# Zeros written at another place, fetched results added by VectorE in a block of its own, and decays of the odd mixer by selectors

## The reference

```
h = x
for layer in (0, 1):                      # first stack
    h += 0.5 * rmsnorm(swiglu(rmsnorm(h)))
    h += rmsnorm(even_mixer(..) if layer == 0 else odd_mixer(..))
    h += 0.5 * rmsnorm(swiglu(rmsnorm(h)))
# second stack, layer 0: modulation (silu(c) @ ada_w), differential attention with
#   rotary q and k over context and latent tokens, dense swiglu of width 3584
# second stack, layer 1: modulation, Fourier mixer, mixture of 8 experts, top 2, width 3584
return rms_norm(x, final_g)
```

```
seg = exp(where(tri, acum[:, :, :, None] - acum[:, :, None, :], -inf))
```

## Time and profile before

| | us |
|---|---|
| median of 3 runs | 2762.97 (2759.33 to 2765.16) |
| the profiled execution | 2765.94 |
| its span | 2764.1 |
| PE busy | 2637.2 (95%) |
| DVE busy | 2058.1 (74%) |
| ACT busy | 1682.6 (61%) |
| POOL busy | 177.5 (6%) |
| mean granted TensorE clock | 0.983 of full speed |

### The profile page before, as it was taken

How to read it: one execution, slowest core, us unless ns; L and a number is a source line. 1 busy time by engine, 2 the same in 40 slices (tenths; PEclk the granted TensorE clock), 3 DMA queues, 4 the chain that set the end, 5 groups by cost and what they waited for, 6 DMA issues and landing times.

```text
span 2764.1 us, 35036 instructions
## 1 busy us (share of the span) xinstructions
PE 2637.2 (95%) x12512; PEld 2162.0 (78%) x12512; DVE 2058.1 (74%) x2379; ACT 1682.6 (61%) x2188; POOL 177.5 (6%) x199
## 2 busy tenths in 40 slices
PE   7999899999999999999986999999999999999997
PEld 6888787888887777888765888788888878888885
DVE  4556667777757765564655785799999999999998
ACT  4446645454457765453552444578788887878885
POOL 2000000000000000004210000200000000000023
PEclk9999999999999999999998999899999999999999
DMA  8555217768744336543148884599999999999995
GB/s 289 183 168 175 92 32 281 240 221 308 243 163 137 122 107 205 183 154 136 46 144 306 309 312 161 178 372 370 378 371 366 387 358 382 367 384 372 367 386 193
DMA packets 284459, 687.41 MB, mean 249 GB/s; under 512 B 13348, under 2 KB 21824, under 8 KB 284352
## 3 DMA queue, kind: packets, MB, share of 16 engines
q1 hardware_dynamic: 266176, 618.65, 62.7%
q0 software_dynamic: 18176, 67.32, 6.8%
HBM read 670.19 MB, written 15.73 MB: 248 GB/s over the span
## 4 chain that ended last, share of the span: by engine, by line
PE 83%; DVE 9%; ACT 4%; issue 4%; DMA 1%; POOL 0%; DVEq 0%; SPq 0%; ACTq 0%
PE ps L2494 25%; PE ps L2496 25%; PE ps L2495 25%; DVE w_lo L1600 3%; PE ps L2642 2%; ACT w_hi L848 1%; PE ps L2726 1%; DVE xt L2376 1%; DVE xn L1679 1%; PE ps L2934 1%; DVE h L1684 1%; PE ps L2957 0%; PE ps L3107 0%; DMA scr<-in_ada_w 0%; DVE act_lo L1668 0%
## 5 line engine op out<-in xcount | busy, mean ns | idle before, releaser
L1600 DVE TENSOR_TENSOR w_lo<-w_raw,w_hi 128x1024 fp32r<-128x1024 f32 x1158 | 1412.1, 1238 | 426.9 <-ACT w_hi L848 395.8
L848 ACT ACTIVATE w_hi<-w_raw 128x1024 fp32r<-128x1024 f32 x1158 | 1211.6, 1057 | 818.0 <-PE ps L2496 817.5
L2494 PE MATMUL ps<-w_hi,act_hi 128*128 128x512 f32 (+1 forms) x3424 | 1350.1, 394 | 75.0 <-DVE w_lo L1600 59.9
L2496 PE MATMUL ps<-w_lo,act_hi 128*128 128x512 f32 (+1 forms) x3424 | 1324.2, 387 | 0.0
L2495 PE MATMUL ps<-w_hi,act_lo 128*128 128x512 f32 (+1 forms) x3424 | 1322.8, 386 | 0.0
L2494 PEld LDWEIGHTS ps<-w_hi,act_hi 128*128 128x128 f32 x3424 | 648.3, 189 | 223.8 <-DVE w_lo L1600 76.2
L2496 PEld LDWEIGHTS ps<-w_lo,act_hi 128*128 128x128 f32 x3424 | 647.9, 189 | 132.6
L2495 PEld LDWEIGHTS ps<-w_hi,act_lo 128*128 128x128 f32 x3424 | 649.2, 190 | 125.0 <-issue 2.9
L1591 DVE SCALAR_TENSOR_TENSOR scr<-scr,small 128x1024 f32<-128x1024 f32 x98 | 125.3, 1278 | 0.0
L1006 ACT ACTIVATE act_hi<-ps 128x512 fp32r<-128x512 f32 (+1 forms) x87 | 62.5, 719 | 64.2 <-PE ps L2642 64.2
L1725 DVE TENSOR_TENSOR act_lo<-ps,act_hi 128x512 fp32r<-128x512 f32 (+1 forms) x87 | 74.0, 850 | 34.7 <-ACT act_hi L1006 34.7
(11 more groups left out here) (509 smaller groups left out, 1457.7 us busy)
## 6 DMA issues: line engine op xcount, KB each, us to landing
w_raw<-in_moe_w SPq DMA_DIRECT2D x337, 1024.0 KB, 7.1
scr<-in_ada_w POOLq DMA_DIRECT2D x48, 1024.0 KB, 6.3
w_raw<-in_ffn_w_gate SPq DMA_DIRECT2D x44, 1024.0 KB, 5.1
w_raw<-in_ffn_w_up SPq DMA_DIRECT2D x44, 1024.0 KB, 5.3
w_raw<-in_ffn_w_down SPq DMA_DIRECT2D x44, 1024.0 KB, 5.0
w_raw<-in_ff_w SPq DMA_DIRECT2D x42, 1024.0 KB, 5.3
w_raw<-in_odd_w_in SPq DMA_DIRECT2D x20, 1024.0 KB, 5.1
w_raw<-in_even_w_in SPq DMA_DIRECT2D x14, 1024.0 KB, 5.2
```

What stands on the lines that cost most here:

```text
L848: act.activation(w_hi[:, g % SPLITS, 0:c * width], w_raw[:, s % RING, o:o + c * width], ACT.Copy).then_inc(hi_done, 1)
L1600: dve.tensor_tensor(w_lo[:, g % SPLITS, 0:c * width], w_raw[:, s % RING, o:o + c * width], w_hi[:, g % SPLITS, 0:c * width].bitcast(F32), ...
L2494: pe.matmul(out_ap, hi, whi, start=start, stop=False)
L2496: return pe.matmul(out_ap, hi, wlo, start=False, stop=stop)
```

## The change

Constants and tiles: `ZEROED` counts nine transfers instead of three, `STORED_AT = 12` is new, `eid` has a 13th entry, `pick` (128 x 64) and `cumr` (128 x 128), both fp32r, are new, some small tiles shrink, `decays_twice` is `sg[:, 0:128]`.

**Zeros.** POOL writes them behind the context's root, ahead of the rotation of keys and queries, from a quarter of a MB of zeroed `lev`. ACT's wait goes.

```diff
             pool.tensor_tensor(rstd[:, 4:6], ..., ALU.pow).then_inc(da_rstd, 1)
+            zeros = lev[:, 0:4, :].rearrange("p c n -> p (c n)")
+            link(pool.memset(zeros, 0.0))
+            for blocks in [rows_in[b:b + 2] for b in range(1, MAX_BLOCKS - 1, 2)] + [rows_in[MAX_BLOCKS - 1:]] + [
+                    rows_out[b:b + 2] for b in range(N_EXPERTS - 2, MAX_BLOCKS, 2)]:
+                flat = blocks.rearrange("b p n -> (b p n)").rearrange("(q j n) -> q j n", q=P, n=BANK)
+                pool.dma_start(flat, bc_mid(zeros, flat.shape[1])).then_inc(rows_moved, 16)
...
-            pool.wait_ge(alo_done, ALO_DENSE)
-            pool.memset(xt[:, 0:DM], 0.0).then_inc(rope_link, 1)
-            pool.wait_ge(rope_link, n(rope_link))
-            for i in range(2):
-                half = rows_in[i * MAX_BLOCKS // 2:(i + 1) * MAX_BLOCKS // 2].rearrange("b p n -> p b n")
-                pool.dma_start(half, bc_mid(xt[:, 0:DM], MAX_BLOCKS // 2)).then_inc(rows_moved, 16)
-            rest = rows_out[N_EXPERTS - 1:].rearrange("b p n -> p b n")
-            pool.dma_start(rest, bc_mid(xt[:, 0:DM], MAX_BLOCKS - N_EXPERTS + 1)).then_inc(rows_moved, 16)
             modulation(1)
```

```diff
+                for k in range(2):
+                    ins = dve.scalar_tensor_tensor(decays_twice[:, 64 * k:64 * k + 64].rearrange("p (b n) -> p b n", b=TB),
+                                                   two(T_DT), -1.0, bc_mid(work[:, 0:32], TB), ALU.mult, ALU.mult)
+                ins.then_inc(dl_g, 1)
+                for k in range(2):
+                    dve.tensor_copy(pick[64 * k:64 * k + 64, :], ident[64 * k:64 * k + 64, 64 * k:64 * k + 64])
...
+                link(dve.tensor_copy(cumr[:], ps[:, 6, 128:256]))
+                dve.tensor_tensor(cumr[64:P, :], ps[64:P, 6, 128:256], cumr[64:P, :].bitcast(F32), ALU.subtract).then_inc(og_la, 1)
...
-                def rows(q, bank):
+                def rows(g, q, bank):
-                    pe.wait_ge(og_la, n(og_la))
+                    pe.wait_ge(og_la, 1)
                     pe.matmul(ps[:, bank, :], identr[:], bc_mid(negr[:], 4), start=True, stop=False)
-                    pe.matmul(ps[:, bank, :], ones, sg[:, 512 * m:512 * m + 512], start=False, stop=True).then_inc(og_R, 1)
+                    for i in range(4):
+                        head = 32 * T + 8 * g + 4 * m + i
+                        ins = pe.matmul(ps[:, bank, i * P:(i + 1) * P], pick[:, head:head + 1].to_broadcast([P, P]), cumr[:],
+                                        start=False, stop=i == 3)
+                    ins.then_inc(og_R, 1)
...
+                pe.matmul(ps[:, 6, 128:256], decays_twice, tri, start=True, stop=True).then_inc(dl_gc, 1)
```

```diff
+                    if s == moe_from + STORED_AT:
+                        sp.wait_ge(mo_y, b + 1)
+                        sp.dma_start(rows_out[bass.ds(b - 1, 1)][0], mo_ye).then_inc(rows_back, 16)
...
-            pool.wait_ge(rows_io, n_blocks * 32)
+            pool.wait_ge(rows_back, last * 16)
...
             for tb in range(TB):
-                step(pool.tensor_scalar(y_first[:, tb, :], y_first[:, tb, :], p_gate[:, tb:tb + 1], None, ALU.mult))
-                step(pool.tensor_scalar(y_second[:, tb, :], y_second[:, tb, :], p_gate[:, 2 + tb:3 + tb], None, ALU.mult))
-                step(pool.tensor_tensor(y_first[:, tb, :], y_first[:, tb, :], y_second[:, tb, :], ALU.add))
-                step(pool.tensor_tensor(y_first[:, tb, :], y_first[:, tb, :], wbc[:], ALU.mult))
-                step(pool.tensor_tensor(h[:, tb, :], h[:, tb, :], y_first[:, tb, :], ALU.add))
+                pool.tensor_scalar(y_first[:, tb, :], y_first[:, tb, :], p_gate[:, tb:tb + 1], None, ALU.mult).then_inc(mo_base, 1)
...
+                def fetched(tb):
+                    y = y_first[:, tb, :]
+                    dve.wait_ge(mo_base, tb + 1)
+                    dve.scalar_tensor_tensor(y, y_second[:, tb, :], p_gate[:, 2 + tb:3 + tb], y, ALU.mult, ALU.add).then_inc(mo_link, 1)
+                def fetched_scaled(tb):
+                    y = y_first[:, tb, :]
+                    dve.wait_ge(mo_link, 2 + 2 * tb)
+                    dve.tensor_tensor(y, y, wbc[:], ALU.mult).then_inc(mo_link, 1)
+                def fetched_added(tb):
+                    dve.wait_ge(mo_link, 3 + 2 * tb)
+                    dve.tensor_tensor(h[:, tb, :], h[:, tb, :], y_first[:, tb, :], ALU.add)
...
+                def moved_and_fetched(i):
+                    if i == GATHERED_AT - 1:
+                        dve.wait_ge(ro_act, 5)
+                        fetched(0)
+                    if i == GATHERED_AT:
+                        fetched_scaled(0)
+                    moved(i)
+                    if i == FF_STEPS - 1:
+                        fetched_added(0)
+                        fetched(1)
+                    if i == FF_STEPS:
+                        fetched_scaled(1)
+                        fetched_added(1)
...
-                with dve.Fori(0, n_blocks) as b:
+                with dve.Fori(0, last) as b:
                     start_blocks(n, b)
-                    gated(FF2, 1, beside)
+                    gated(FF2, 1, moved)
                     lo_ahead(2)
                     end_blocks(n)
+                gp[0], ahead[0], n.at = first_gran, first_ahead, first_at
+                start_blocks(n, last)
+                gated(FF2, 1, moved_and_fetched)
+                lo_ahead(2)
```

More of the change, by code:

```diff
@@ L604, in _ @@
                     sp.wait_ge(rows_moved, SCATTERED)
-                    for half in (slice(0, BANK), slice(BANK, DM)):
-                        sp.dma_start(mo_rows[:, half], rows_in[1][:, half]).then_inc(rows_io, 16)
+                    sp.dma_start(mo_rows, rows_in[1]).then_inc(rows_io, 16)
             sp.wait_ge(mo_ids, n(mo_ids))
@@ L1734, in gated @@
                         hidden(i - 1)
-                    if beside and i in (CONTEXT_AT, GATHERED_AT):
+                    if beside and i:
                         beside(i)
@@ L2110, in odd @@
                 link(dve.scalar_tensor_tensor(dtw[:, T_DT, :], dtw[:, T_X, :], 0.0, dtw[:, T_LN, :], ALU.max, ALU.add))
-                dve.scalar_tensor_tensor(two(T_A), two(T_DT), -1.0, bc_mid(work[:, 0:32], TB), ALU.mult, ALU.mult).then_inc(dl_g, 1)
+                dve.scalar_tensor_tensor(two(T_A), two(T_DT), -1.0, bc_mid(work[:, 0:32], TB), ALU.mult, ALU.mult)
+                for k in range(2):
[4 more added lines that the diff above has]
+                    dve.tensor_copy(pick[64 * k:64 * k + 64, :], ident[64 * k:64 * k + 64, 64 * k:64 * k + 64])
                 lo(1)
@@ L2430, in experts @@
+                last = dve.value_load(eid[0:1, 12:13], min_val=N_EXPERTS - 1, max_val=N_EXPERTS + MAX_EXTRA - 1)
+                first_gran, first_ahead, first_at = gp[0], ahead[0], dict(n.at)
+                with dve.Fori(0, last) as b:
+                    start_blocks(n, b)
+                    gated(FF2, 1, moved)
                     lo_ahead(2)
                     end_blocks(n)
-                dve.wait_ge(ro_act, 5)
+                gp[0], ahead[0], n.at = first_gran, first_ahead, first_at
@@ L2433, in experts @@
+                start_blocks(n, last)
+                gated(FF2, 1, moved_and_fetched)
+                lo_ahead(2)
+                n.block = None
                 dve.wait_ge(ctx_in, 48)
-                dve.wait_ge(mo_base, n(mo_base))
                 dve.wait_ge(mo_end, n(mo_end))
@@ L3007, in odd @@
                 pe.matmul(ps[:, 6, 0:64], tri, dtw[:, T_A, :], start=True, stop=True)
-                pe.matmul(ps[:, 6, 64:128], ones, dtw[:, T_A, :], start=True, stop=True).then_inc(dl_gc, 1)
+                pe.matmul(ps[:, 6, 64:128], ones, dtw[:, T_A, :], start=True, stop=True)
+                pe.matmul(ps[:, 6, 128:256], decays_twice, tri, start=True, stop=True).then_inc(dl_gc, 1)
                 for g in range(3):
@@ L3018, in beside_x @@
                                 pe.wait_ge(og_e, 4 * g)
-                            rows(0, 4)
-                            rows(1, 5)
+                            rows(g, 0, 4)
+                            rows(g, 1, 5)
                             pe.wait_ge(cv_act, CV + 2 * (3 + g))
@@ L3040, in beside_z @@
                                 pe.wait_ge(og_lo, 2 * g - 1)
-                            rows(2, 4)
+                            rows(g, 2, 4)
                             from_state(g)
@@ L3046, in beside_z @@
                                 pe.wait_ge(og_lo, 2 * g)
-                            rows(3, 5)
+                            rows(g, 3, 5)
                         if k == 3:
@@ L3058, in odd @@
                 pe.wait_ge(og_e, 12)
-                rows(0, 4)
-                rows(1, 5)
+                rows(3, 0, 4)
+                rows(3, 1, 5)
                 pe.wait_ge(proj_out, 8 + 11)
@@ L3081, in odd @@
                 pe.wait_ge(og_lo, 6)
-                rows(2, 4)
-                rows(3, 5)
+                rows(3, 2, 4)
```

(1 more changed line is left out.)

57 lines of the change are left out of this document (22 added, 35 removed).

## The result

The changed kernel takes 2712.28 us (median of 4 runs, 2709.26 to 2714.96) against 2761.15 for the kernel before (4 runs, 2758.75 to 2765.16): ratio 0.9818, 95% interval 0.9807 to 0.983, that is 48.9 us less. The forecast was 2716.3, or 46.7 less than a kernel before at 2762.97. The profiled execution took 2714.96, span 2712.8: 51.3 less than the span before.

The account below looks back on a forecast made before the run. PE bounds the kernel, matmuls being 83% of the span. Zeros -29.3, odd decays -10.7 and fetched results -6.7 sum to -46.7 us, from the runs' median 2762.97 to 2716.3 us; range 2707 to 2733.

Parts of the forecast that it names:

- Zeros, -29.3: Dense stage start: ada_w page lands in time, PE's 27.7 us wait and 1.6 of slow clock go; ends 24 and 30.
- The price 0 at the new place: Behind the context's root, from about 1067 us: zeros cost PE nothing, the seven-page weight ring covering them; upper end 21 us.
- 31 us for the zeros, or 52 beside the weights: New place: 8704 KB take 31 us with the engines alone, 52 with weights at 334 GB/s in all.
- my rule, 1 us for each beyond 31: New place: where the weight ring's cover is gone, each us of zeros beyond 31 costs PE 1 us.
- rival D: New place: zeros shut weights out, running under 114 GB/s, kernel slower than before; 2784 us at 90 GB/s; chance 0.03.
- Odd decays, -10.7: Odd mixer: four single-pass selector matmuls replace DVE products and an f32 matmul, shortening PE's work and a stall; ends -2, -13.
- my -3.6, -2.5 and +1.2: Behind the odd mixer's third group: stall gone 3.6 us, slow clock gone 2.5, ACT's late copy of x costs 1.2.
- Rival A: Odd mixer: selector matmuls run at f32's rate, four taking 0.86 us; total gain 40 us, 2723 us; chance 0.2.
- Fetched results, -6.7: Last expert block: POOL's arithmetic moves to DVE, regaining 10.7 us of PE waits and losing 4.0; ends -10.7, -3.
- 10.7 less 3.0 for the rest of the new work: Last block: 10.7 us regained; 1.3 lost at step 5, 1.4 at step 6, 0.3 from POOL's two multiplies.
- Rival C: Last block: POOL's two remaining multiplies hold DVE 7.9 us, leaving this gain at 0 to 1 us; 2722 us; chance 0.1.
- part 3: Last expert block: the fetched results done by DVE instead of POOL, forecast at -6.7 us.

Follow-up runs that it names:

- e2_decays: Kernel before with only the odd decays changed, made by the turned product and selectors: 2749.8 us, 13.2 less.
- experiment 9: Changed kernel with the 16 DVE products put back and PE waiting for two of them behind the third group: 2720.1 us, ratio 0.9844.
- Experiment 11: Changed kernel with last block's rows stored at page 8 instead of 12, six DVE instructions paired at steps 3, 4 and 6: 2710.9 us, ratio 0.9803.
- experiment 4: Kernel before with the same three transfers of zeros issued behind the first two ada_w pages instead of in front: 2755.4 us, 7.6 less.
- experiment 6: Changed kernel with each of the nine transfers of zeros issued twice, 17.8 MB instead of 8.9: 2713.8 us, ratio 0.9827.
- experiment 5: Kernel before with the same three transfers of zeros at about the same time, issued from SP's queue instead of POOL's: 2739.9 us, 21.7 less.

## Why the prediction was right, step by step

**Zeros, -29.3.** The stretch gave 29.1, and 29.8 in the kernel with this part alone. The page was in time, the 27.7 and the slow clock behind them went; the 3.93 us were nine matmuls and not ten, so the slow clock was worth 1.9, not 1.6. The price 0 at the new place held, but by another way than I had worked out, and that is luck. I took 31 us for the zeros, or 52 beside the weights. That 52 holds the weights of 41 us only; 334 GB/s less the 204 of the weights leaves 130, and makes it 68 us. They flowed for some 70 us, the issues alone over 63, with POOL standing still for 6.3 to 11.4 us before the next. By my rule, 1 us for each beyond 31, that is 39 us of idle; PE had none. Rule and rival D both priced slow zeros as if weights were shut out for as long, but beside them the weights landed in 6.7 to 7.9 us by the median: a slow transfer leaves more to the others. At 8.9 MB in some 70 us, 127 GB/s and not far above D's 114, PE lost nothing, and neither with twice the bytes.

**Odd decays, -10.7.** 10.4 in the profiled pair, 10.7 in e2_decays. A group takes 34.05 us instead of 35.72: 1.67 each, 5.0 in three, as forecast. Behind group three a wait alone makes 5.5 (experiment 9); my -3.6, -2.5 and +1.2 give 4.9. ACT's copy of x was 1.12 late for 1.2. Rival A's price was 6.7, measured 6.3; it failed on the rate alone. The selector matmul took 0.098 for the 0.11 that I took from 32 columns. The Trainium skill, "TensorE: Matmul & The Clock Gate", section "Wait — 56ns, not 53.3ns?", puts warm bf16 matmuls of 128 columns 56 ns apart; that does not carry over to these fp32r matmuls with a new stationary each, which the trace has 98 ns apart.

**Fetched results, -6.7.** Measured 6.2 to 6.3, and two misses, of 3.1 and of 2.6 us, nearly cancel in it. DVE found everything ready at step 4, so its new wait cost nothing. The end cost 4.1 where I had put 1.0. PE already waited 1.6 for DVE there before the change, so the pair behind the last w_lo went on the path whole (2.4 of waiting; I had set it against the last transposes only), and behind the longer wait the slow clock took 1.7 more, a term that I did not have. Experiment 11 takes both back. Up to the last weight matmul the block is 10.3 us shorter (130.9 to 120.5 behind the eviction), where 10.7 less 3.0 for the rest of the new work, 7.7, was forecast. The new work cost little there: 1.7 of waits over an ordinary block's 0.8, of which 1.1 at step 5 for 1.3 and 0.6 for the pair at step 6 for 1.4. So taking POOL's arithmetic away gave about 12 by estimate (10.3 and 1.7), more than the 10.7 that I had from the list of waits, which shows only 8.8 of the 10.3 (a wait is counted from the end of a pipelined matmul, 0.39 behind its start where the next could start after 0.23). Small slips of mine: 11.3 less 0.8 is 10.5, not 10.6; the 1.21 of the earlier trace rows is a median, and one w_lo in that line took 2.05; rows 16 give 120.83 and not 120.87.

Rival C: DVE is not shut out by the multiplies that stay. The Trainium skill, "SBUF — State Buffer", section "SBUF: two separate sides", would have it locked out by their read of SBUF for a whole instruction, 4.0 us here; the rows agree by two w_lo in six, lengthened by 0.7 and 0.8 us, and disagree by the rest (1.21 to 1.23).

**The rest.** 46 of the 48.9 us are in the three stretches. Of the 5.5 between the profiles beyond them 3.2 are slow spells that only one of them has, 2.9 lie where the lost clock is 3.3 less, and -0.7 stand in front of the odd mixer. The forecast of 46.7 for the three parts is nearer to their 45.8 than the sum of its terms deserves. Whether the 2 to 3 us by which the medians go beyond the stretches are slow spells too was not settled.

## What to carry to other kernels

A bulk transfer has two prices: its bytes on the DMA engines, which buffered weights hid here even at double size, and its place in an engine's queue, where it holds up the engine itself and every small load behind it; look first at what is issued behind it, and at the idle time in front of each issue. Before a stall is priced, find every later item of the same queue that someone waits for, not only the first. Work put behind the last weight of a kernel counts whole if the end already waits for that engine, and here more than whole, by the slow clock behind the longer wait; the same instructions spread over earlier steps were nearly free. Where a sum comes true, check its terms: within part 3 they were off by 3.1 and 2.6 us in opposite directions.

## What the hardware showed that I had not expected

- POOL stands still while it issues large transfers in a row: 12.2 and 11.9 us before the second and third (experiment 4; 3072, 3072 and 2560 KB), 9.2 to 12.0 in the kernel before, 4.9 to 11.4 between those of 1024 KB (the changed kernel and experiment 6). SP issued the same three in experiment 5 in 7.9 us, as its timeline shows, with a stop only at the third:

```profile
1431.47 1.07 SPq L610 DMA_DIRECT2D rows_in<-xt  x2
1432.58 6.74 SPq L612 DMA_DIRECT2D rows_out<-xt  x1
```

- An idle of 1.5 us of PE is followed by a slow spell, a mean granted clock of 0.76 to 0.79 over 4 us, in five of the fourteen traces and by 1.00 in the others, with the same instructions there, at 1.6 us each time; two such places behind the odd mixer make up 3.2 us between the two profiles.
- PE's last eight matmuls take 3.67 us at a granted clock of 1.00 in the six traces where the wait in front of them is 1.6 us, and 5.2 to 5.4 (0.58 in the first 4 us of the changed kernel's) in the eight where it is 4.0.
- At 128 columns with a new stationary for each, a pass takes 0.10 us in fp32r and 0.11 in f32, hardly less than one of 256 columns (0.12).
